# Two decoder blocks on one core: the rotary half exchange by 32-partition transfers, its products on GpSimd

## What is computed

```
def apply_rope(t, cos, sin):
    half = t.shape[-1] // 2
    t1, t2 = t[..., :half], t[..., half:]
    return jnp.concatenate([t1 * cos - t2 * sin, t2 * cos + t1 * sin], axis=-1)

def mla_mixer(h, w_q_a, q_a_norm_g, w_q_b, w_out, k_nope, k_rope, v, cos, sin):
    c_q = rms_norm(h @ w_q_a, q_a_norm_g)
    q = (c_q @ w_q_b).reshape(B, S, MLA_HEADS, QK_NOPE_DIM + QK_ROPE_DIM)
    q_nope = q[..., :QK_NOPE_DIM]
    q_rope = apply_rope(q[..., QK_NOPE_DIM:], cos[:, None, :], sin[:, None, :])
    # logits: (q_nope . k_nope + q_rope . k_rope) * scale, causal softmax, times v
    return ctx.reshape(B, S, MLA_HEADS * V_HEAD_DIM) @ w_out
```

## Time and profile before

| | us |
|---|---|
| median of 3 runs (1144.2 to 1145.61) | 1145.58 |
| the profiled execution | 1143.81 |
| its span | 1142.0 |
| TensorE busy in the span | 1125.8 |
| VectorE busy | 866.2 |
| ScalarE busy | 653.0 |
| GpSimd busy | 265.1 |

### The profile page before, as it was taken

How to read it: one execution, slowest core, us unless ns; L and a number is a source line. 1 busy time by engine, 2 the same in 40 slices (tenths; PEclk the granted TensorE clock), 3 DMA queues, 4 the chain that set the end, 5 groups by cost and what they waited for, 6 DMA issues and landing times.

```text
span 1142.0 us, 26248 instructions
## 1 busy us (share of the span) xinstructions
PE 1125.8 (99%) x9706; PEld 1102.6 (97%) x9706; DVE 866.2 (76%) x1387; ACT 653.0 (57%) x1075; POOL 265.1 (23%) x256
## 2 busy tenths in 40 slices
PE   8999999999999999999999999999999999999997
PEld 8998999999998999999999999999999999999997
DVE  6876877766697877756677489999767788999854
ACT  6666656544447656644555566666555455666543
POOL 0001400012230600011200263444321024454421
PEclk9999999999999999999999999999999999999999
DMA  9643666555643666565465245664566655565461
GB/s 303 211 148 108 193 197 193 194 186 182 166 140 110 189 199 202 165 206 184 147 188 161 95 160 174 200 203 152 190 201 210 206 187 184 190 209 181 152 202 61
DMA packets 213136, 203.51 MB, mean 178 GB/s; under 512 B 11840, under 2 KB 212800, under 8 KB 213072
## 3 DMA queue, kind: packets, MB, share of 16 engines
q1 hardware_dynamic: 212928, 202.44, 55.7%
q10 hardware_dynamic: 144, 0.20, 0.1%
HBM read 201.57 MB, written 1.05 MB: 177 GB/s over the span
## 4 chain that ended last, share of the span: by engine, by line
PE 94%; DVE 3%; ACT 1%; issue 1%; DMA 0%; POOL 0%; DVEq 0%; ACTq 0%; SPq 0%; POOLq 0%
PE gemm L718 28%; PE gemm L720 28%; PE gemm L719 27%; PE gemm L729 2%; PE gemm L731 1%; PE gemm L730 1%; DVE w_lo L1652 1%; PE score L925 1%; PE gemm L937 1%; DMA x<-in_xT 0%; PE score L1062 0%; ACT act_a L1298 0%; PE trans L890 0%; PE misc L756 0%; ACT w_hi L1280 0%
## 5 line engine op out<-in xcount | busy, mean ns | idle before, releaser
L1652 DVE TENSOR_TENSOR w_lo<-w_raw,w_hi 128x1024 fp32r<-128x1024 f32 (+2 forms) x404 | 480.3, 1195 | 143.6 <-ACT w_hi L1280 141.7
L1280 ACT CAST w_hi<-w_raw 128x1024 fp32r<-128x1024 f32 (+2 forms) x404 | 402.3, 1002 | 148.1 <-PE gemm L720 141.0
L718 PE MATMUL gemm<-act_a,w_hi 128*128 128x256 f32 (+1 forms) x1704 | 472.2, 277 | 2.7 <-DVE act_a L1661 1.7
L720 PE MATMUL gemm<-act_a,w_lo 128*128 128x256 f32 (+1 forms) x1704 | 469.1, 275 | 0.0
L719 PE MATMUL gemm<-act_a,w_hi 128*128 128x256 f32 (+1 forms) x1704 | 469.1, 275 | 0.0
L718 PEld LDWEIGHTS gemm<-act_a,w_hi 128*128 128x128 f32 (+1 forms) x1704 | 318.4, 187 | 7.1 <-DVE w_lo L1652 3.5
L719 PEld LDWEIGHTS gemm<-act_a,w_hi 128*128 128x128 f32 (+1 forms) x1704 | 318.5, 187 | 0.4
L720 PEld LDWEIGHTS gemm<-act_a,w_lo 128*128 128x128 f32 (+1 forms) x1704 | 318.4, 187 | 0.3
L718 PE MATMUL gemm<-hid,w_hi 128*128 128x256 f32 x864 | 238.1, 276 | 0.0
L719 PE MATMUL gemm<-hid,w_hi 128*128 128x256 f32 x864 | 237.7, 275 | 0.0
L720 PE MATMUL gemm<-hid,w_lo 128*128 128x256 f32 x864 | 237.7, 275 | 0.0
(11 more groups left out here) (278 smaller groups left out, 1400.0 us busy)
## 6 DMA issues: line engine op xcount, KB each, us to landing
w_raw<-in_ffn_w_up SPq DMA_DIRECT2D x76, 1024.0 KB, 5.2
w_raw<-in_ffn_w_down SPq DMA_DIRECT2D x32, 1024.0 KB, 5.0
w_raw<-in_gla_w_in SPq DMA_DIRECT2D x12, 1024.0 KB, 5.4
w_raw<-in_ffn_w_down SPq DMA_DIRECT2D x16, 768.0 KB, 4.2
w_raw<-in_sc_w_in SPq DMA_DIRECT2D x12, 1024.0 KB, 5.2
w_raw<-in_fox_w_in SPq DMA_DIRECT2D x10, 1024.0 KB, 6.9
w_raw<-in_ffn_w_down SPq DMA_DIRECT2D x16, 640.0 KB, 3.9
w_raw<-in_fox_w_out SPq DMA_DIRECT2D x4, 1024.0 KB, 4.9
```

Source lines behind the costliest of these rows:

```text
L718: nc.tensor.matmul(ps, wh[:, k, cols], act[:, k0 + k, 0, :], start=start and k == 0, stop=False)
L720: last = nc.tensor.matmul(ps, wl[:, k, cols], act[:, k0 + k, 0, :], start=False, stop=stop and k == nk - 1)
L1280: nc.scalar.copy(split_half(w_hi, nc_, nj), raw_half(nc_, nj)).then_inc(w_hi_ready, 1)
L1652: nc.vector.tensor_tensor(split_half(w_lo, nc_, nj), raw_half(nc_, nj), split_half(w_hi, nc_, nj).bitcast(F32), ALU.subtract).then_inc(w_l ...
```

## The change

The five exchange matmuls and their matrix go. ScalarE issues four transfers of 32 partitions by 256 values (32 KB) for each tile instead, from the raw tile to a new tile `m_rot`; the sign lies in the sine table. GpSimd makes the cosine and the sine product of a tile, in the groups (0), (1, 2), (3, 4), all cosine products of a group before its sine products. VectorE only adds, rope 0 and 1 before `m_q` 0 and 1, ropes 2, 3 and 4 one by one later. The scores of heads h and h + 1 wait for the key and for the query tiles up to their own. The constants are 128 columns shorter (64 KB less to load), and the tiles behind the shared area move as its end is the largest of all its uses.

```diff
--- before.py
+++ after.py
@@ constants
-    at("sin", 256)[:] = np.tile(np.sin(ang).T, (4, 1))
-    half = ROPE // 2
-    for m in range(P):
-        if m % ROPE < half:
-            at("rot", 128)[m + half, m] = -1.0
-        else:
-            at("rot", 128)[m - half, m] = 1.0
+    at("sin", 256)[:] = np.tile(np.sin(ang).T, (4, 1)) * np.where(i % ROPE < ROPE // 2, -1.0, 1.0)[:, None]
@@ tiles and semaphores
+        m_rot = sb("m_rot", [P, 5, T])
-        rot_place = [b[:, 0:T] for b in (trans, misc, score[1], trans, misc)]
-        rot_done = sem("rot_done")
+        rot_landed = [sem(f"rot_landed{n}") for n in range(5)]
+        rope_sin = sem("rope_sin")
@@ GpSimd
-            for n in range(5):
-                pool.wait_ge(dve_evac, DE["KVQ"] + 5 if n == 0 else DE["QR"] + n)
-                if n == 0:
-                    pool.wait_ge(act_ready, AT["lat"] + 5)
-                nc.gpsimd.tensor_tensor(m_lat[:, n, :], m_kr_raw[:] if n == 0 else m_qr_raw[:, n - 1, :], cos_t,
-                                        ALU.mult).then_inc(rope_cos, 1)
+            def rope_products(tiles):
+
+                for n in tiles:
+                    pool.wait_ge(dve_evac, DE["KVQ"] + 5 if n == 0 else DE["QR"] + n)
+                    if n == 0:
+                        pool.wait_ge(act_ready, AT["lat"] + 5)
+                    nc.gpsimd.tensor_tensor(m_lat[:, n, :], m_kr_raw[:] if n == 0 else m_qr_raw[:, n - 1, :], cos_t,
+                                            ALU.mult).then_inc(rope_cos, 1)
+                for n in tiles:
+                    pool.wait_ge(rot_landed[n], 64)
+                    nc.gpsimd.tensor_tensor(m_rot[:, n, :], m_rot[:, n, :], sin_t, ALU.mult).then_inc(rope_sin, 1)
+
+            rope_products((0,))
+            rope_products((1, 2))
+            rope_products((3, 4))
@@ TensorE
-            def rotate(n):
-
-                src = m_kr_raw[:] if n == 0 else m_qr_raw[:, n - 1, :]
-                pe.wait_ge(dve_evac, DE["KVQ"] + 5 if n == 0 else DE["QR"] + n)
...
-                if n >= 3:
-                    pe.wait_ge(rope_step, 2 * (n - 3) + 1)
-                nc.tensor.matmul(rot_place[n], rot, src, start=True, stop=True).then_inc(rot_done, 1)
-
@@ mla_scores
-                pe.wait_ge(rope_step, 6 if h == 0 else 10)
+                pe.wait_ge(rope_step, h // 2 + 2)
@@ TensorE's order
             q_half("QR", 0)
-            rotate(0)
             q_half("QR", 1)
-            rotate(1)
-            rotate(2)
             for s in range(MLA_H + 4):
...
-                if s == 0:
-                    rotate(3)
-                    rotate(4)
@@ ScalarE
+            def rotate(n):
+
+                act.wait_ge(dve_evac, DE["KVQ"] + 5 if n == 0 else DE["QR"] + n)
+                src = m_kr_raw[:] if n == 0 else m_qr_raw[:, n - 1, :]
+                for to, frm in ((0, 32), (32, 0), (64, 96), (96, 64)):
+                    act.dma_start(m_rot[to:to + 32, n, :], src[frm:frm + 32, :]).then_inc(rot_landed[n], 16)
+
+            rotate(0)
             prep(C0["KB"], 0)
             root("q_a")
             prep(C0["KB"], 1)
             for j in range(2):
                 prep(C0["QR"], j)
+            rotate(1)
+            rotate(2)
             for s in range(MLA_H + 5):
                 if s < 6:
                     prep(C0["QA"] + s // 2, s % 2)
+                if s == 0:
+                    rotate(3)
+                    rotate(4)
@@ VectorE
                 dst = m_kr[:] if n == 0 else m_qr[:, n - 1, :]
-                dve.wait_ge(rot_done, n + 1)
-                nc.vector.tensor_tensor(dst, rot_place[n], sin_t, ALU.mult).then_inc(rope_step, 1)
-                dve.wait_ge(rope_step, 2 * n + 1)
                 dve.wait_ge(rope_cos, n + 1)
-                nc.vector.tensor_tensor(dst, dst, m_lat[:, n, :], ALU.add).then_inc(rope_step, 1)
+                dve.wait_ge(rope_sin, n + 1)
+                nc.vector.tensor_tensor(dst, m_rot[:, n, :], m_lat[:, n, :], ALU.add).then_inc(rope_step, 1)
...
                 if s == 0:
-                    for n in range(3):
-                        rope(n)
+                    rope(0)
+                    rope(1)
...
-                if s == 0:
-                    rope(3)
-                    rope(4)
+                if s < 3:
+                    rope(s + 2)
```

More of the change, by code:

```diff
@@ L87 @@
 for _name, _n in [("ones", 128), ("ident", 128), ("mask", 256), ("tri", 512), ("tri_chunk", 128), ("cos", 256),
-                  ("sin", 256), ("rot", 128), ("chunk_mask", 128), ("pick", FOX_H),
+                  ("sin", 256), ("chunk_mask", 128), ("pick", FOX_H),
                   ("head_row", GLA_H * GLA_H)]:
@@ L200, in build @@
         inv_sum = sb("inv_sum", [P, 3, 2])
-        assert used[0] <= end_hid
+        end_fox = used[0]
         overlay()
@@ L218, in build @@
         m_inv = sb("m_inv", [P, 3, 2])
-        assert used[0] <= end_hid
+        end_mla = used[0]
         overlay()
@@ L239, in build @@
         overlay()
-        used[0] = max(end_hid, end_gla)
+        used[0] = max(end_hid, end_fox, end_mla, end_gla)
         g_up = sb("g_up", [GATE_RANK, 512])
@@ L269, in build @@
         head_row = con[:, CON["head_row"]:CON["head_row"] + GLA_H * GLA_H]
-        rot = con[:, CON["rot"]:CON["rot"] + 128]
         chunk_mask = con[:, CON["chunk_mask"]:CON["chunk_mask"] + 128].bitcast(U32)
```

## The result

| | before | after |
|---|---|---|
| median of 8 runs, same chip (us) | 1144.89 | 1147.74 |
| lowest to highest | 1144.02 to 1147.24 | 1147.17 to 1150.31 |
| ratio, with its 95% interval | | 1.0028 [1.0020, 1.0037] |

The change costs 0.28% by the ratio, which is 3.2 us (the two medians differ by 2.85); the forecast was a gain of 0.8 us. The median of after lies inside the forecast's range of 1142.9 to 1148.0, but on the other side of before. The profiled execution of after took 1150.31 us, the highest of its eight. Its busy times and its chain stand against the earlier trace rows: TensorE is busy 3.4 us longer with ten records fewer, and transfers and waits have entered the chain.

A forecast was written before the change was run, and what follows sets the result against it. TensorE, busy 99%, was taken as the bound, with VectorE also full in the rotary stage. A 2.15 us ceiling, cut by waiting for transfers, left 0.8 us off the median 1145.58: 1144.8 us, range 1142.9 to 1148.0.

The forecast's parts named there:

- Landing: Rotary transfers ahead of rope(1): 2.4 us to land, taken from the output's store, bounds 2.2 and 5.5; landed at 336.55.
- rival A: Transfers land late at rope(1): 0.8 us slower (1146.4) at q_b's medians, 3.9 us slower (1149.5) at its maxima; chance 0.20.
- Issue: ScalarE's DMA issues for rotate(1): 0.44 us each, the fourth starting at 334.15; bounds 0.37 and 0.99.
- Sine, rope(1), `m_q`: After landing: sine product on GpSimd 0.73 us, to 337.3; then rope(1) and two m_q on VectorE, scores at about 338.5.
- A wait there holds everything that is queued behind it on VectorE.: At rope(1), a wait also holds two m_q, rope(2), VB 1's low half, m_q 2 and 3, rope(3) and the maxima.
- The ceiling: Most that removing TensorE's rotations could gain at the first scores: 2.15 us, from the floor.
- floor of 337.15: Earliest start of the first scores without rotations on TensorE, 337.15 instead of 339.30, after QA half 1 ends.
- 0.5 us of bound: Collision of sine product 0 on GpSimd with a low half on VectorE: taken as 0, at most 0.5 us.
- rival D: VectorE's new collisions with cosine products 3 and 4 and the sine products take back the 0.8 us: 1145.6; chance 0.14.
- 3 us of slack: First exponential on ScalarE follows its DMA issues at about 343.0 against 342.76, with 3 us to spare before the transposes.
- Rival C: ScalarE's queue of 16 issues before the first exponential becomes the bound from 0.66 us an issue; 1146.9 at 0.74; chance 0.07.
- Finer waits alone: Scores waiting for one rope pair at a time: 0 alone, but keep rope(2) to rope(4) off the path.

The follow-up runs named there:

- the load held: The changed kernel with SyncE's second 1 MB load of output weights held until all five rotary tiles have landed; ratio to before 0.9997, median 1144.34 us.
- filled wait: The changed kernel with 26 idle-filling TensorE matmuls ahead of the first scores; ratio to before 1.0028, median 1148.88 us.
- run without exchange: The changed kernel without the transfers, so no half exchange, GpSimd multiplying the unexchanged tile by the sine; ratio to before 0.9998, median 1145.03 us.

## Why the prediction was wrong

1. **Landing, the step that failed.** "Landing. [...] I take 2.4, since 32 KB is nearer to the store's time without a queue". It measured 4.21, and 1.91 with the load held. The bounds were 2.2 and 5.5, so the value was inside; the choice went by the size of the transfer, where it had to go by what else is on the engines at that time. The argument against rival A, "32 KB each, on ScalarE's own queue", is no argument: that queue moved nothing before 338.5 us, while SyncE's moved 0.91 MB over the same engines. The Trainium skill, "DMA: Bandwidth & Descriptors", section "Issuing engines are not separate DMA queues", states that DMAs of all issuing engines run on the same 16 DMA engines. It also says that they interleave; in this trace they did so only as the load drained. The 2.1 us that the prediction worked out from the section "Anatomy of one DMA", whose figures are for DMAs issued by GpSimd, is near the quiet case (1.9) and far from the one beside the load.
2. **Issue.** 0.44 taken from one DMA, 0.61 measured; three of them make 0.5 us. With 1.8 for the landing that is 2.3 of the 2.4 us by which the scores missed the forecast (12.82 instead of 10.42 after QR half 0).
3. **Sine, rope(1), `m_q`.** 0.73 and 1.2 by forecast (337.3 to 338.5), 0.73 and 1.24 measured (341.65 to 342.89). Right.
4. **"A wait there holds everything that is queued behind it on VectorE."** Right: 4.08 us of idle VectorE, released by GpSimd. The wait was foretold, its price wasn't.
5. **The clock.** Rival A was priced as a shift (0.8 us at medians, 3.9 at maxima). The scores came 1.6 late, between the two, and the half clock behind the wait, which no term had, added 2.8 in the profiled run. The ratio's 3.2 us would be 1.6 for the wait and about 1.7 for one half-clock stretch in a typical run. The run times at equal mean clock bear out the 1.6; the 1.7 is argued from their steps, and the filled wait, which took the half clock away in its trace, didn't take it out of the ratio.
6. **The ceiling.** 2.15 by the floor of 337.15; by the run without exchange 1.45 at the scores, 1.36 of stage, and nothing in the ratio. The floor had no term for rope sums that meet GpSimd's products; the 0.5 us of bound was for the low half beside sine product 0. Only rival D named such collisions.
7. **ScalarE and the maxima.** "3 us of slack" was right for the quiet case only in part: with the load held for all, ScalarE is 0.76 us late at the second head's transposes, which had no term. Rival C, the queue of issues, exists at this size.
8. **Finer waits alone.** 0 in the sum. No run tested it by itself; nothing here speaks against it.

So the mechanism of rival A held and was given 0.20; slower should have had the larger part. That the median of after still lies in the range is luck in part: the range reached up to rival A's prices, and the measured loss is made of a smaller wait than its maxima and of half clock, which no rival had.

## What to carry to other kernels

Price a small transfer by the traffic at the microsecond of its issue, in windows as narrow as the transfer, and not by the mean of a stage. Before an exchange leaves TensorE, look at which engine will wait for it and what stands behind that wait in the same order; let it carry only tiles that have slack of a full landing beside a load (4 to 6 us here) and keep the first one where it was, or hold the load back until the transfers are in. Of four stalls of TensorE here, of 2.59, 3.42, 3.55 and 3.71 us, three came with half clock behind them, at some 1.5 us to 2.8 us on top. And compare runs at equal mean clock where the gain is as small as one half-clock stretch.

## What was not expected of the hardware

- 32 KB from SBUF to SBUF: 1.8 to 1.9 us at the median on quiet engines, with single ones up to 3.5; the fourth transfer of tile 1 took 4.2 to 4.9 beside a 1 MB load; 128 KB in one transfer 5.9 beside it.
- While the load ran, ScalarE's queue moved no packet from 335 to 338.5 us, with six transfers issued by then.
- One issue of such a transfer holds ScalarE's queue for 0.51 to 0.61 us, up to 1.64 at the most, where the load of the vectors took 0.44.
- A rope sum with both inputs in SBUF takes 0.95 us beside GpSimd's products and 0.41 alone.
- Half-clock stretches of about 3.4 us come behind some waits and not behind others, and also where TensorE had been busy without a gap for 12 us (no exchange, 656.5 to 660 us). They shift single runs by steps of about 1.7 us.
